# Two norms of a two-block transformer forward: VectorE adds the squares, TensorE sums over features twice instead of eight times

## The reference, cut to what matters

```python
def _rmsnorm(x, g):
    xf = x.astype(jnp.float32)
    y = xf * lax.rsqrt(jnp.mean(xf * xf, axis=-1, keepdims=True) + EPS)
    return (y * g.astype(jnp.float32)).astype(x.dtype)

def second_block(x, mem, norm_g, mem_norm_g, w_in, ...):
    for l in range(DEPTH):                       # DEPTH = 2
        h = _rmsnorm(x, norm_g[l])
        z = h @ w_in[l]
        ...
        mem_kv = _rmsnorm(mem, mem_norm_g[l]) @ w_mem_kv[l]
        ...
        x = x + u @ w_out[l]
    return x
```

## Time and profile before

| what | value |
|---|---|
| median of 3 runs | 3045.16 us (3045.05 to 3052.68) |
| profiled execution, its own time | 3052.64 us |
| profiled execution, span | 3051.2 us |
| TensorE (PE) busy | 3015.6 us, 99% |
| TensorE weight loads (PEld) | 2517.8 us, 83% |
| GpSimd (POOL) busy | 1934.4 us, 63% |
| VectorE (DVE) busy | 1472.7 us, 48% |
| ScalarE (ACT) busy | 792.6 us, 26% |
| chain that ended last | PE 94%, DVE 2%, POOL 2% |

### The profile page before, as it was taken

The page is one execution under the profiler, slowest core; times in us unless marked ns, Lnnn a source line. Parts: engine busy times, 40 slices in busy tenths (PEclk is TensorE's granted clock), DMA queues, the critical chain, the costliest instruction groups (busy, mean ns, idle before and its releaser), DMA issues.

```text
span 3051.2 us, 41829 instructions
## 1 busy us (share of the span) xinstructions
PE 3015.6 (99%) x15554; PEld 2517.8 (83%) x15554; DVE 1472.7 (48%) x2995; ACT 792.6 (26%) x1727; POOL 1934.4 (63%) x2202
## 2 busy tenths in 40 slices
PE   9999999999999999999999999999999999999999
PEld 8888887888888878888888887888888887888887
DVE  2333334467740583777314746663233463664332
ACT  1111111222210352222113116552102213654110
POOL 5555555589987787999776762225777484122775
PEclk9999999999999999999999999999999899999999
DMA  4222222123232222223323221011333231001222
GB/s 153 92 92 92 85 91 92 56 83 97 97 99 96 74 86 74 97 97 97 110 97 125 90 83 36 23 35 63 98 121 103 88 97 63 29 29 34 92 97 90
DMA packets 66872, 255.71 MB, mean 84 GB/s; under 512 B 7664, under 2 KB 8176, under 8 KB 64880
## 3 DMA queue, kind: packets, MB, share of 16 engines
q1 hardware_dynamic: 62496, 227.57, 22.6%
q10 hardware_dynamic: 4176, 25.47, 2.3%
HBM read 250.91 MB, written 2.10 MB: 83 GB/s over the span
## 4 chain that ended last, share of the span: by engine, by line
PE 94%; DVE 2%; POOL 2%; issue 1%; ACT 1%; DMA 0%; ACTq 0%; POOLq 0%; DVEq 0%
PE bank L363 24%; PE bank L365 24%; PE bank L364 24%; PE bank L1844 4%; PE bank L1829 2%; PE bank L1818 2%; PE bank L403 2%; PE bank L655 1%; PE bank L390 1%; PE bank L395 1%; PE bank L391 1%; PE bank L1813 1%; POOL w_lo L2187 1%; PE bank L1555 1%; PE bank L1295 1%
## 5 line engine op out<-in xcount | busy, mean ns | idle before, releaser
L2187 POOL TENSOR_TENSOR w_lo<-w_raw,w_hi 128x256 fp32r<-128x256 f32 x1736 | 1400.7, 838 | 36.2
L2183 POOL TENSOR_SCALAR w_hi<-w_raw 128x1024 fp32r<-128x1024 f32 x434 | 491.3, 1132 | 1049.8 <-PE bank L365 936.7
L363 PE MATMUL bank<-in_hi,w_hi 128*128 128x512 f32 x1408 | 554.8, 394 | 0.8 <-POOL w_lo L2187 0.5
L365 PE MATMUL bank<-in_hi,w_lo 128*128 128x512 f32 x1408 | 548.6, 390 | 0.0
L364 PE MATMUL bank<-in_lo,w_hi 128*128 128x512 f32 x1408 | 547.8, 389 | 0.0
L363 PE MATMUL bank<-z_hi,w_hi 128*128 128x512 f32 x976 | 392.6, 402 | 0.0
L365 PE MATMUL bank<-z_hi,w_lo 128*128 128x512 f32 x976 | 381.3, 391 | 0.0
L364 PE MATMUL bank<-z_lo,w_hi 128*128 128x512 f32 x976 | 380.8, 390 | 0.0
L365 PEld LDWEIGHTS bank<-in_hi,w_lo 128*128 128x128 f32 x1408 | 264.2, 188 | 55.7
L363 PEld LDWEIGHTS bank<-in_hi,w_hi 128*128 128x128 f32 x1408 | 264.5, 188 | 53.8 <-issue 0.9
L364 PEld LDWEIGHTS bank<-in_lo,w_hi 128*128 128x128 f32 x1408 | 264.6, 188 | 52.9
(11 more groups left out here) (433 smaller groups left out, 5065.5 us busy)
## 6 DMA issues: line engine op xcount, KB each, us to landing
w_raw<-in_units SPq DMA_DIRECT2D x434, 512.0 KB, 3.4
bias<-in_bias ACTq DMA_DIRECT2D x8, 1152.0 KB, 5.2
o_all<-in_cmp_w ACTq DMA_DIRECT2D x4, 2048.0 KB, 8.3
x_res<-in_x ACTq DMA_DIRECT2D x4, 512.0 KB, 8.9
mem_in<-in_mem ACTq DMA_DIRECT2D x2, 1024.0 KB, 8.7
out<-x_res ACTq DMA_DIRECT2D x4, 512.0 KB, 2.6
consts<-in_consts ACTq DMA_DIRECT2D x1, 710.5 KB, 3.8
both_layers_cols<-in_layer_cols ACTq DMA_DIRECT2D x2, 140.5 KB, 5.6
```

The source lines that it names most:

```text
L363: pe.matmul(out, hi[:, w], rh, start=start and n == 0, stop=False)
L365: last = pe.matmul(out, lo[:, w], rh, start=False, stop=stop and n == len(tiles) - 1)
L2183: d = c.s.unit_hi.on(pool.tensor_scalar(c.w_hi[s][:, :], c.w_raw[s][:, :], 1.0, 0.0, ALU.mult, ALU.add))
L2187: last = pool.tensor_tensor(c.w_lo[s][:, w], c.w_raw[s][:, w], c.w_hi[s][:, w].bitcast(F32), ALU.subtract)
```

## The change

For the two norms (a flag `added=True`) VectorE adds the squares of chunks 1 to 6 into the buffer of chunk 0, one addition for each chunk right behind that chunk's low part. TensorE sums nothing for chunks 0 to 6; at chunk 7's place it waits for the addition of chunk 6, sums buffer 0, waits for the squares of chunk 7, and sums those. ScalarE's squares of the memory get a third buffer, and from chunk 3 on it waits for an addition (`squares_added` of chunk k - 2) instead of a sum. Block one's norms and the norm of layer 0's `x` stay as they were.

```diff
+    def square(self, k):
+        n = len(self.sq)
+        return self.sq[k % n if not self.added or not k else 1 + (k - 1) % (n - 1)]
...
-        self.mem_sq = [a.take(f"mem_square{j}", [P, M]) for j in range(2)]
+        self.mem_sq = [a.take(f"mem_square{j}", [P, M]) for j in range(2)] + [Area(self.nc, at - 2048).take("mem_square2", [P, M])]
...
 def pe_norm_sum(pe, c, z, k):
+    if z.added and k < DC - 1:
+        return
+    b = c.bank[z.banks[0]]
+    if z.added:
+        pe.wait_ge(*c.s.squares_added[z.name, DC - 2])
+        pe_sum_tokens(pe, c, b, z.square(0), z.n_tiles, True, False, (z.name, 0))
     pe.wait_ge(*c.s.squared[z.name, k])
-    pe_sum_tokens(pe, c, c.bank[z.banks[0]], z.sq[k % len(z.sq)], z.n_tiles, k == 0, k == DC - 1, (z.name, k))
+    pe_sum_tokens(pe, c, b, z.square(k), z.n_tiles, k == 0, k == DC - 1, (z.name, k))
...
 def act_norm_chunk(act, c, z, k):
-    if k >= len(z.sq):
+    if z.added and k >= len(z.sq):
+        act.wait_ge(*c.s.squares_added[z.name, k - len(z.sq) + 1])
+    elif k >= len(z.sq):
         act.wait_ge(*c.s.tokens_summed[z.name, k - len(z.sq)])
...
 def dve_norm_chunk(dve, c, z, k):
     dve.wait_ge(*c.s.hi_done[z.name, k])
     c.s.lo_done.on(dve.scalar_tensor_tensor(z.lo[:, k, :], ...), (z.name, k))
+    if z.added and 0 < k < DC - 1:
+        total = z.square(0)[:, 0:z.n]
+        dve.wait_ge(*c.s.squared[z.name, k])
+        if k > 1:
+            dve.wait_ge(*c.s.squares_added[z.name, k - 1])
+        c.s.squares_added.on(dve.tensor_tensor(total, total, z.square(k)[:, 0:z.n], ALU.add), (z.name, k))
```

More of the change, by code:

```diff
@@ L159, with __init__ @@
 class Norm:
-    def __init__(self, name, src, gain, hi, lo, sq, r, n_tiles=TT, banks=(7, 6), heads=False):
+    def __init__(self, name, src, gain, hi, lo, sq, r, n_tiles=TT, banks=(7, 6), heads=False, added=False):
+        self.added = added
         self.name, self.src, self.gain, self.hi, self.lo, self.sq, self.r = name, src, gain, hi, lo, sq, r
@@ L318, in layer_norm @@
     def layer_norm(self, layer):
-        return Norm(("z", layer), self.x, self.cols[:, layer, C_NORM:C_NORM + DC], self.zh, self.zl, self.z_sq, self.zr, heads=True)
+        return Norm(("z", layer), self.x, self.cols[:, layer, C_NORM:C_NORM + DC], self.zh, self.zl, self.z_sq, self.zr, heads=True, added=layer == 1)
     def memory_norm(self, layer):
         return Norm(("mem", layer), self.mem, self.cols[:, layer, C_MEMNORM:C_MEMNORM + DC], self.mh, self.ml, self.mem_sq, self.mem_r,
-                    MT, banks=(4, 4), heads=True)
+                    MT, banks=(4, 4), heads=True, added=True)
 KINDS = [("v", 0), ("v", 1), ("v", 2), ("q", 0), ("k", 0), ("q", 1), ("k", 1), ("q", 2), ("k", 2)]
@@ L469, in act_norm_chunk @@
     c.s.hi_done.on(act.activation(z.hi[:, k, :], z.src[:, k, :], ACT.Copy, scale=z.gain[:, k:k + 1]), (z.name, k))
-    if k >= len(z.sq):
+    if z.added and k >= len(z.sq):
+        act.wait_ge(*c.s.squares_added[z.name, k - len(z.sq) + 1])
+    elif k >= len(z.sq):
         act.wait_ge(*c.s.tokens_summed[z.name, k - len(z.sq)])
-    c.s.squared.on(act.activation(z.sq[k % len(z.sq)][:, 0:z.n], z.src[:, k, :], ACT.Square), (z.name, k))
+    c.s.squared.on(act.activation(z.square(k)[:, 0:z.n], z.src[:, k, :], ACT.Square), (z.name, k))
 def act_norm_wide(act, c, z):
```

## The result

The changed kernel takes **3054.4 us** (median of 20 runs), the kernel before, on the same chip, 3047.56 (20 runs). The ratio is 1.0024, 95% interval 1.0018 to 1.0031: by that ratio 7.3 us slower, between 5.5 and 9.4 (the two medians lie 6.8 apart). That is within 0.3% of no change, and its sign is sure. One execution of the 20 took 8006.48 us and is no part of the comparison. The profiled execution of after has a span of 3052.0 us; the one of before had 3051.2.

A forecast was written before the change was run, and what follows sets the result against it. TensorE, busy 99% of the span, was taken to bound the kernel. The terms -5.5 - 5.3 + 14.2 + 0.8 + 4.0 gave +8.2 us on the median 3045.16, so 3053.4 us, range 3048 to 3063.

The forecast's parts named there:

- (a): Layer 1's norm of x: TensorE's sums for six of eight chunks go, 0.92 us each, -5.5 us.
- (b): The memory's norm: TensorE's sums for three chunk pairs (m = 5, 6, 7) go in each layer, -5.3 us.
- The wait at m = 8: TensorE idles for VectorE's addition of chunk 6, queued behind other work: 7.1 us in each layer, +14.2 us.
- The small wait: TensorE waits at m = 8 for ep_sq, as ScalarE's squares now wait for additions: 0.4 us per layer, +0.8 us.
- The clock: Half clock on TensorE after the idle time at m = 8: 2.0 us in each layer, +4.0 us.
- The sum: All removed and added terms together, over the whole kernel: +8.2 us, giving 3053.4 us on the median.
- main case: All terms hold, with the idle time at m = 8 and its clock price: 3053.4 us, likely 3050 to 3057, chance 0.58.
- The loss at L1555: Rival: the median run also has the slow small instructions and half clock at L1555: 3060.5 us, chance 0.26.
- The rival on the other side: At m = 8 chunk 6's addition is done in time and TensorE does not wait: 3035.2 us, chance 0.05.
- GpSimd held up: Rival: VectorE's additions stop GpSimd's weight splits and TensorE waits for weights: up to 11.8 us more, 3065.2, chance 0.03.

The follow-up runs named there:

- the second run: Changed kernel with the additions for layer 1's x only, the memory's norm as before, repeated on another chip: 3041.01 us, ratio 0.9972 to the kernel before.
- memory_early_no_x: Changed kernel with VectorE's memory steps at the head of m = 7 and 8, without the additions for x: 3041.55 us, ratio 0.998 to the kernel before.
- memory_first: Changed kernel, but at m = 8 VectorE makes its two memory steps ahead of its compressed step: 3039.15 us, ratio 0.9981 to the kernel before.
- memory_early: Changed kernel with VectorE's memory steps ahead of all other work at m = 7 and 8: 3034.55 us, ratio 0.9953 to the kernel before.
- after_again: The changed kernel itself, unaltered, run again on another chip: 3055.89 us, ratio 1.0026 to the kernel before.
- filled_wait: Changed kernel with 28 unneeded 512-column matmuls in front of TensorE's wait at m = 8: 3049.84 us, ratio 1.0002 to the kernel before.
- mem_only: Changed kernel with the additions for the memory's norms only, none for layer 1's x: 3063.71 us, ratio 1.006 to the kernel before.
- wait_alone: Kernel before, without additions, but TensorE's sum of the memory's chunk 6 waits for VectorE's low part: 3069.06 us, ratio 1.0071.
- z_only: Changed kernel with the additions for layer 1's x only, the memory's norm as before: 3041.31 us against 3044.95, ratio 0.9981.

## Why the prediction was right, and where not

Predicted were 3053.4 us as +8.2 on the median; measured +7.3 by the ratio, and 3054.4, in the range. That 3054.4 is only 1.0 from the forecast is helped by two errors against each other: the kernel before has 3047.56 as the median of 20 runs, 2.4 more than the 3045.16 of three runs that the sum started from, and the change is smaller than the +8.2.

- **(a), -5.5 us:** 5.50 in the trace; alone -5.8 and, in the second run, -8.5 us (5.2 to 11.6); with the half clock taken off -5.2 and -5.7. Right, also in that the additions cost nothing here, though one took 1.23 us (six instructions, median; longest 1.53), above the 1.21 at most of the earlier trace rows.
- **(b), -5.3 us:** measured by memory_early_no_x, -6.1 (1.8 to 10.4), and -5.9 with the half clock taken off. Right.
- **The wait at m = 8, +14.2:** 2 x 6.8 = 13.6, in the place, behind the engine and for the reason given. The addition took 0.42 us where I took 0.48. Right. memory_first and memory_early show that it is VectorE's order: moving the two steps shortens it to 1.25 us, and moving them further ahead removes it.
- **The small wait, +0.8:** 0.4. Right in place, half in size.
- **The clock, +4.0, "between 0 and 3.3" in each layer:** this is the step that was mis-sized. It measured 3.3 and 3.7, 7.0 together (trace of after), 6.6 (after_again), 7.3 (filled_wait). I had allowed up to 3.3 in each layer and taken 2.0. I had taken from the gap at 1131 to 1137 us that the half clock ends 4.9 us after the engine resumes; here it lasted 7.1 and 7.9 us, and after the same gap in after_again and mem_only 5.7 to 7.6. The length so differs between executions of the same instructions; what decides it was not tried. The Trainium skill (TensorE: Matmul & The Clock Gate, section "Why this matters for your kernels") advises against idle gaps between bursts of matmuls, since the clock drops back. This case's runs agree: an idle time of 6.4 us alone (wait_alone) brought 3.2 us of loss in each layer, and matmuls put into the gap (filled_wait) took it away.
- **The sum** would with the clock term of after's trace alone put right have been +11.2, and with all terms as measured +10.2, above the measured interval (5.5 to 9.4). That the forecast lay so near is in part luck: the clock term was 3 us too small, and what makes the times 3 us closer than the two traces was not foreseen. Part of it is that one pair of traces is one draw: with the clock terms of after_again (6.6) or mem_only (5.8) the sum is +9.8 or +9.0. Another explanation is not shown: the executions of before would hold more half-clock stretches that come by chance (its 20 runs spread over 11.4 us), and the waits at m = 8 would swallow some that fall there, as in z_only's profile. The lowest times, 10.0 us apart, speak for it; on the chip of after_again the clocks hardly do, since its 23.9 us less 10.2 for the two stretches at the gaps leave 13.7, where before has 14.3.
- **The ends of the main case's own range** are each 0.2 us too low as added up: -10.8 + 15.8 + 3.0 + 6.6 is +14.6 and not +14.4, and the low end +5.6 and not +5.4. Nothing hangs on it.
- **The loss at L1555** (rival, 0.26): after's profile has it in neither layer, before's has it; it comes and goes, as the prediction held. In filled_wait it stood in m = 9 of layer 0. The rival's time did not come.
- **The rival on the other side** (TensorE does not wait, 3035.2): not what after does, but memory_early makes it true, with 3034.55. **GpSimd held up:** in the two changed stretches of after TensorE waits for no split; not seen. Where VectorE and GpSimd worked at the same time, now one was stretched and now the other: in memory_first VectorE's addition took 0.94 us instead of 0.42, in memory_early GpSimd's instruction 1.85 instead of 0.74. TensorE paid for the first of these, in the 1.25 us gap.
- **The chances:** the most likely case came, the signs of all its terms are right, and the ratio ended just below the 0.3% line, which I held a little less likely than above it.

## What to carry to other kernels

Before work is moved from the engine that sets the pace to one that is half idle, look not at the idle engine's load but at its queue: a 0.4 us instruction behind 6 us of others, of which the first waits for the busy engine, gave back all that 18 of them saved. Moving the producer up in its engine's order turned +7.3 us into -14.3 (-11.3 with the half clock taken off, all that the removed sums are worth). A gap on TensorE can cost more than its length: here 6.4 to 6.8 us of gap cost another 2.7 to 3.7. And where single times scatter by more than the effect, the granted clock of each execution can take most of the scatter out.

## What the runs showed of the hardware

- TensorE's half clock (1.2 GHz) after a gap of 6.8 us lasted 7.1 and 7.9 us from the resuming in after, 5.7 to 7.6 in after_again and mem_only, where the 5 us gap of the earlier trace rows had 4.9. At a gap of 1.25 us, among sums of one or two columns, it was there three times of four, for 3.4 or 6.8 us.
- Half-clock stretches also came with no wait, in other places in each execution: 3.4 us from 46.5 us in after and at m = 8 in z_only; 10 us from 15 us in before; beside the 62-column matmuls at L1555, 11.2 us instead of 7.2.
- A 128x256 addition on VectorE took 0.42 us alone (after) and 0.94 beside GpSimd's split (memory_first), the low part 0.48 and 1.26. In memory_early the addition took 0.41 beside the split, and GpSimd's instruction 1.85 instead of 0.74.
